# One decoder layer on one core: two weight splits behind a sigmoid, one low part behind three sums, five convolution taps ahead of the row copies

## The chip, the cores and the metric

The kernel runs on one core of a Trainium2 chip. The metric is the device time of one execution in microseconds (us), the median over several runs. Engines are named as the profile names them: PE (TensorE, matmuls), DVE (VectorE), ACT (ScalarE), POOL (GpSimd) and SP (SyncE, which issues the loads).

## The reference

One layer of a decoder for 512 prompt tokens and 64 sample tokens (8 sequences of 8), all in one pass, 576 tokens in all. Everything is in 32-bit floats.

```python
x = x + 0.5 * swiglu_ffn(x, norm_ffn1, ffn1_w_gu, ffn1_w_down)
h = rmsnorm(x, norm_mix)
glu_in, q_a, c_kv, k_pe, gate_a, gate_b = split(h @ w_in)
u = ga * sigmoid(gb)                    # the two halves of glu_in
y_conv = conv_branch(u, ...)            # causal depthwise conv (31 taps), layernorm, silu, projection
y_attn = latent_attention(q_a, c_kv, k_pe, cached pages) @ w_attn_out
m = sigmoid(gate_a) * y_conv + sigmoid(gate_b) * y_attn
x = x + m @ w_out
x = x + 0.5 * swiglu_ffn(x, norm_ffn2, ffn2_w_gu, ffn2_w_down)
```

D_MODEL is 1024, D_FF 2816, the convolution has 512 channels, the latent part of `w_in` 672 columns and each gate 1024.

## The kernel before

Activations stand transposed, channels on the 128 partitions and the 576 tokens along the row, in two halves of 288. A product of 32-bit values is made from three faster ones: each operand is split into a high part and a low part (the rest), and PE adds high x high, high x low and low x high.

**Chunks.** The weights come in tiles of 128 columns, called chunks: SP loads one into one of four raw buffers (`load_chunk`), ACT copies it into one of two high buffers (`split_hi`, L442 to 447), POOL subtracts that from the raw tile in four pieces, which gives the low part (`split_lo`, L454), and PE makes 48 matmuls of it (`chunk`, `product`, L468). `split_hi` of chunk n waits until PE has used chunk n-2, since there are two high buffers. PE's next chunk waits for the low part and for one of four pairs of PSUM banks, which is free when DVE has read the result of four units before (`unit_read`).

**The mixing stage.** The chunks of `w_in` follow each other without a pause: eight for the GLU (`n_glu`, pairs j = 0 to 3), six for the latent rows (`n_lat`), sixteen for the gates (`n_gate`). For each GLU pair DVE scales both results out of PSUM (`scaled`, L1861), ACT applies the sigmoid (`glu`, L1024) and DVE multiplies. After that come `sample_conv` (for the sample tokens: one product of 1984 elements per partition, L2087, and a sum, L2089) and taps of the prompt convolution (`taps`, L2071 and L2074), which DVE has to do at some time and which are dealt out between the other steps. The numbers `AT_LAT`, `AT_GATE` and `AT_GATE2` say which tap comes where: five behind each of the gates 0 to 6, five in another place (below), four behind each of the last four gates. For a gate DVE scales the result, ACT applies the sigmoid (`gate`, L1039).

Behind gate 7 PE transposes the latent rows back in five groups of six (L1477, 128 tokens each, the last 64), each into its own pair of banks; DVE copies each out (L2160, L2161). The fifth group needs the pair that the first row copy frees, gate 8's chunk the one of the second. Then POOL fills `lat_ss`, ACT squares and sums the rows (L1065, L1066), DVE makes the norms, and the gates 8 to 11 run beside it.

**The feed-forward stages.** The first three pairs of columns run as plain chunks. The other nineteen, called units, are made from seven products of half size instead of eight (L1390, twelve matmuls each, in the order GATE1, GATE2, SUM_G, SUM_U, DIF, REST, UP2). For each unit SP loads the gate columns (`w_raw`, L573) and the up columns (`up_rows`, L578); DVE makes four sums of them (`weight_sums`, `last_weight_sum`, L1817 to L1827); ACT makes the high parts (`weight_hi`, L896); DVE makes the low parts of GATE1, GATE2, SUM_G (`weight_low`, L1911) and of UP2 (`up2_low`, L1917), POOL the others (L730). `combine` adds the seven results. All of DVE's work on unit u+1 is dealt out between the `combine`s of unit u; for unit 0 this order is written out in `first_seven`. There is one `up_rows` buffer: SP's load of it for unit u+1 waits for `up2_low` of unit u, and in SP's queue the gate columns of unit u+2 stand behind that load.

```python
if not first or u or f:
    sp.wait_ge(up2_lo, unit_sums(f, u, 1, 0))
for half, k0 in enumerate((0, KH)):
    dst = up_rows[:, half, :].rearrange("p (k c) -> p k c", c=P)
    sp.dma_start(dst, wv[:, k0:k0 + KH, ds(of(u, P, PLAIN[f] * P + DFF), P)]).then_inc(up_in, 16)
```

**The cached pages.** Behind the attention of the prompt SP issues 16 loads of `c_nat` and 16 of `kpe_nat` for the first sequence. The first wait for `prep_q`, which DVE signals with `rope_rep`.

Of the kernel before, what the change touches and what calls it, by code (L numbers as in the profile page):

```python
# [22 lines left out]
P = 128  # L23
D = 1024
KD = D // P
# [21 lines left out]
LATC = -(-LAT // P)  # L47
# [13 lines left out]
RAWS, HIS = 4, 2  # L61
# [32 lines left out]
def layer(nc, x_prompt, x_sample, cache_ckv, cache_kpe, state_conv, page_table, w, const, out):  # L94

    ctx = ExitStack()
    with ctx:
# [255 lines left out]
        GLU_TAPS, LAT_TAPS, GATE_TAPS, GATE2_TAPS = 4, 5, 5, 4  # L353
        AT_LAT = (CT - 1) * GLU_TAPS
        AT_GATE = AT_LAT + (LATC - 1) * LAT_TAPS
        AT_GATE2 = AT_GATE + KD * GATE_TAPS
# [9 lines left out]
        n_lat = n_glu + 2 * CT  # L366
# [29 lines left out]
        def of(u, m, c):  # L396

            return m * u + c if isinstance(u, int) else u[0] * (2 * m) + (m * u[1] + c)
# [6 lines left out]
        def unit_sums(f, u, m, c):  # L405

            return of(u, m, m * U0[f] + c)
# [9 lines left out]
        def seven_bank(f, slot):  # L417

            return (4 + IN_ORDER.index(slot)) % 8
# [18 lines left out]
        def arrived(n, r):  # L438

            return 32 * (n // RAWS + 1) if isinstance(n, int) else (n - r) * (32 // RAWS) + 32  # L440

        def split_hi(act, n, r, size, free=True):  # L442

            act.wait_ge(w_in_sem[r], arrived(n, r))
            if free:
                act.wait_ge(w_used, n - (HIS - 1))
            act.activation(w_hibuf[:, r % HIS, 0:size], w_rawbuf[:, r, 0:size], ACT.Copy).then_inc(w_hi_done, 1)  # L447
# [391 lines left out]
        def _(act):  # L839
# [182 lines left out]
            def glu(j):  # L1022
                act.wait_ge(unit_read, glu_base(j) + 2 * j + 2)
                act.activation(tb[:, :], tb[:, :], ACT.Sigmoid).then_inc(sigmoid_done, 1)  # L1024

            for j in range(CT - 1):
                if j:
                    up_hi(n_glu, j + 1, j + 1)
                glu(j)
            for n in (n_lat, n_lat + 1):  # L1030
                split_hi(act, n, n % RAWS, KD * P)
            glu(CT - 1)
            for c in range(2, LATC):
                n = n_lat + c
                split_hi(act, n, n % RAWS, KD * min(P, LAT - c * P))

            def gate(g, q0=q_gate):
                act.wait_ge(unit_read, g + (q0 + 1))
                act.activation(gates[:, ds(g, 1), :], gates[:, ds(g, 1), :], ACT.Sigmoid).then_inc(sigmoid_done, 1)  # L1039

            def gate_hi(g, gmod):
                split_hi(act, g + n_gate, (n_gate + gmod) % RAWS, KD * P)

            gate_hi(0, 0)
            gate_hi(1, 1)
            with act.Fori(0, KD // 4) as i:
                for c in range(4):
                    gate_hi(i * 4 + (c + 2), c + 2)
                    gate(i * 4 + c)

            steps = [0]

# [9 lines left out]
            for i in range(NT):  # L1062
                n = P if i < PT_TILES else TS
# [12 lines left out]
            for i in range(NT):  # L1076
                n = P if i < PT_TILES else TS
# [707 lines left out]
        def _(dve):  # L1785
# [65 lines left out]
            for g in range(NX):  # L1851
                n = X_GROUPS[g][1]
# [60 lines left out]
            def up2_low(f, u, b):  # L1913

                dve.wait_ge(w7_sum, unit_sums(f, u, 4, 1))
                dve.wait_ge(w7_hi, unit_sums(f, u, 7, HI_ORDER.index(UP2) + 1))
                dve.tensor_tensor(w7[b][:, UP2, 1, :], up_rows[:, 1, :], w7[b][:, UP2, 0, :].bitcast(F32), ALU.subtract).then_inc(up2_lo, 1)  # L1917

            def combine(f, u, slot):

                n = IN_ORDER.index(slot) + 1
                dve.wait_ge(w7_used, unit_sums(f, u, 7, n))
                got = ps[:, seven_bank(f, slot), 0:HALF]
                lo, hi = slice(0, HALF), slice(HALF, T)
                if slot == GATE2:
                    dve.wait_ge(part_read, unit_sums(f, u, 1, 1))
                    dve.wait_ge(a_made, of(u, 1, FT * f + PLAIN[f]))
                    dve.tensor_tensor(ta[:, lo], got, parts[:, 1, :], ALU.add).then_inc(c_done, 1)
                elif slot == SUM_G:
                    dve.tensor_tensor(parts[:, 2, :], got, parts[:, 1, :], ALU.add).then_inc(c_done, 1)  # L1930
                elif slot == SUM_U:
                    dve.wait_ge(c_done, unit_sums(f, u, 7, 2))
                    dve.tensor_tensor(parts[:, 0, :], got, parts[:, 2, :], ALU.add).then_inc(c_done, 1)
                elif slot == DIF:
                    dve.wait_ge(c_done, unit_sums(f, u, 7, 3))
                    dve.tensor_tensor(tb[:, hi], got, parts[:, 0, :], ALU.add).then_inc(c_done, 1)
                    dve.tensor_tensor(parts[:, 2, :], got, parts[:, 2, :], ALU.add).then_inc(c_done, 1)
                elif slot == REST:
                    dve.tensor_tensor(ta[:, hi], got, parts[:, 0, :], ALU.add).then_inc(c_done, 1)
                else:  # L1940
                    dve.wait_ge(c_done, unit_sums(f, u, 7, 5))
                    dve.tensor_tensor(tb[:, lo], got, parts[:, 2, :], ALU.add).then_inc(c_done, 1)
# [25 lines left out]
            def first_seven(f):  # L1968

                weight_sums(f, 1, 1)  # L1970
                weight_low(f, 1, 1, GATE1)
                up2_low(f, 1, 1)
                combine(f, 0, GATE2)
                last_weight_sum(f, 1, 1)
                weight_low(f, 1, 1, GATE2)
                combine(f, 0, SUM_G)
                weight_low(f, 1, 1, SUM_G)
                combine(f, 0, SUM_U)
                combine(f, 0, DIF)
                combine(f, 0, REST)  # L1980

# [111 lines left out]
            def taps(n0, n1):  # L2093

                for n in range(n0, n1):
                    if n % W == 0:
                        dve.wait_ge(ext_done, n // W + 1)
                    tap(n // W, n % W, n if n % W else None)
# [37 lines left out]
            def gate(g, q):  # L2136

                dve.wait_ge(w_used, n_gate + g + 1)
                scaled(gates[:, g, :], q % 4).then_inc(unit_read, 1)
                if g < KD - 1:  # L2140
                    taps(AT_GATE + GATE_TAPS * g, AT_GATE + GATE_TAPS * (g + 1))
                elif g >= KD + 4:
                    taps(AT_GATE2 + GATE2_TAPS * (g - KD - 4), AT_GATE2 + GATE2_TAPS * (g - KD - 3))

            for c in range(8):
                gate(c, q_gate + c)
# [9 lines left out]
            for i in range(NT):  # L2156
                n = P if i < PT_TILES else TS
# [1 line left out]
                dve.wait_ge(tr_done, KD + 4 + i)  # L2159
                dve.tensor_copy(lat[0:n, i, 0:512], ps[0:n, 2 * s, :])  # L2160
                dve.tensor_copy(lat[0:n, i, 512:LAT], ps[0:n, 2 * s + 1, 0:LAT - 512]).then_inc(unit_read, 1)  # L2161
            taps(AT_GATE + GATE_TAPS * (KD - 1), AT_GATE2)
            gate(KD, q_gate2)
            dve.wait_ge(filled, 3)
            dve.wait_ge(ss_done, NT)
# [20 lines left out]
            for i in range(NT):  # L2186
                n = P if i < PT_TILES else TS
                dve.tensor_scalar(lat[0:n, i, 0:QL], lat[0:n, i, 0:QL], lat_ss[0:n, 0, i:i + 1], None, ALU.mult)
                c = lat[0:n, i, QL:QL + KL]
# [5 lines left out]
            for i in range(NT):  # L2195
                n = P if i < PT_TILES else TS
# [9 lines left out]
            for i in range(NT):  # L2206
                n = P if i < PT_TILES else TS
# [392 lines left out]
```

## Time and profile before

| | |
|---|---|
| median of 3 runs | 1602.19 us (1600.95 to 1603.7) |
| the profiled execution | 1603.7 us, of it span in the trace 1601.9 us |
| PE busy | 1572.9 us, 98% of the span |
| DVE, ACT, POOL busy | 1043.6, 628.3, 575.4 us (65%, 39%, 36%) |
| mean granted clock of PE | 0.995 |
| loaded from HBM | 117.79 MB, 76 GB/s over the span with what is written |

The span is that of one execution, taken by the hardware profiler; the time of the run is a little longer. Busy shares are means over all stages. Times in the text such as "at 480.32" are microseconds from the start of the span. Ends of matmuls are modelled, so two rows that follow each other may overlap by 0.15 us.

### The profile page before, as it was taken

How to read it: one execution, taken by the hardware profiler on the slowest of the kernel's cores; microseconds unless marked ns; L12 is line 12 of the kernel's file. 1: busy time of each engine (PE TensorE's matmuls, PEld its weight loads, DVE VectorE, ACT ScalarE, POOL GpSimd, SP SyncE). 2: the span in 40 equal slices, each digit the busy share in tenths (PEclk: the TensorE clock that was granted, in tenths of full speed). 3: DMA queues.
4: the chain of work that ended last, by engine and by line, in shares of the span. 5: the costliest groups of instructions: out<-in, count | busy, mean ns of one | idle time of the engine just before them, and what ended most of it. 6: DMA issues, size and time to landing. Idle time of an engine off the chain costs nothing.

```text
span 1601.9 us, 32058 instructions
## 1 busy us (share of the span) xinstructions
PE 1572.9 (98%) x11330; PEld 1495.8 (93%) x11330; DVE 1043.6 (65%) x1674; ACT 628.3 (39%) x1168; POOL 575.4 (36%) x604
## 2 busy tenths in 40 slices
PE   9999999999999999998999999999999999999997
PEld 8999999999999998687988888888999999999997
DVE  4998888521279966664877777774549988884001
ACT  5443435322221241363544445552335444353110
POOL 2065555454446644220000000002561654554441
PEclk9999999999999999998999999999999999999999
DMA  5133334232233421002122222211231332342321
GB/s 158 51 99 99 91 92 125 63 91 73 78 85 104 122 70 56 1 2 66 53 61 60 59 59 53 53 42 53 84 111 56 93 105 83 100 115 65 89 73 59
DMA packets 230106, 122.24 MB, mean 76 GB/s; under 512 B 28255, under 2 KB 227015, under 8 KB 230004
## 3 DMA queue, kind: packets, MB, share of 16 engines
q1 hardware_dynamic: 229182, 120.56, 26.8%
q8 instruction: 52, 0.85, 0.2%
q10 hardware_dynamic: 830, 0.48, 0.1%
q14 instruction: 42, 0.34, 0.1%
HBM read 117.79 MB, written 3.58 MB: 76 GB/s over the span
## 4 chain that ended last, share of the span: by engine, by line
PE 85%; DVE 8%; issue 3%; ACT 2%; SPq 1%; DVEq 0%; DMA 0%; POOL 0%; ACTq 0%; POOLq 0%
PE ps L468 38%; PE ps L1390 25%; PE ps L1703 8%; PE ps L1641 4%; PE ps L1275 1%; PE ps L1501 1%; DVE xs L1905 1%; PE ps L1627 1%; PE ps L1526 1%; PE ps L1508 1%; DVE page_ss L2498 1%; PE ps L1551 1%; SPq L657 1%; SPq L660 1%; ACT sq L1196 1%
## 5 line engine op out<-in xcount | busy, mean ns | idle before, releaser
L454 POOL TENSOR_TENSOR w_lobuf<-w_rawbuf,w_hibuf 128x256 fp32r<-128x256 f32 (+2 forms) x336 | 313.8, 965 | 360.1 <-ACT w_hibuf L447 360.1
L1390 PE MATMUL ps<-xs,w 128*128 128x288 f32 x3192 | 429.4, 296 | 5.7 <-DVE w L1911 4.5
L1390 PEld LDWEIGHTS ps<-xs,w 128*128 128x128 f32 x3192 | 427.0, 188 | 7.8 <-issue 7.8
L730 POOL TENSOR_TENSOR w<-w_raw,w 128x256 fp32r<-128x256 f32 x216 | 219.7, 1049 | 233.9 <-DVE w_raw L1821 153.1
L447 ACT ACTIVATE w_hibuf<-w_rawbuf 128x1024 fp32r<-128x1024 f32 (+1 forms) x90 | 104.8, 1164 | 357.4 <-PE ps L468 356.6
L2045 DVE SCALAR_TENSOR_TENSOR xT<-ps,xT 128x576 f32<-128x576 f32 x24 | 18.2, 758 | 228.5 <-PE ps L468 228.5
L468 PE MATMUL ps<-a_hi,w_lobuf 128*128 128x288 f32 x704 | 152.2, 297 | 0.0
L468 PE MATMUL ps<-a_hi,w_hibuf 128*128 128x288 f32 x704 | 152.1, 296 | 0.0
L468 PE MATMUL ps<-a_lo,w_hibuf 128*128 128x288 f32 x704 | 150.3, 294 | 0.0
L468 PE MATMUL ps<-x_hi,w_hibuf 128*128 128x288 f32 (+1 forms) x672 | 145.7, 298 | 1.1 <-DVE cT L2202 0.7
L468 PE MATMUL ps<-x_lo,w_hibuf 128*128 128x288 f32 (+1 forms) x672 | 144.2, 296 | 0.0
L468 PE MATMUL ps<-x_hi,w_lobuf 128*128 128x288 f32 (+1 forms) x672 | 144.1, 296 | 0.0
L896 ACT ACTIVATE w<-w_raw 128x512 fp32r<-128x512 f32 x228 | 128.2, 622 | 10.9 <-DVE w_raw L1817 5.8
L1703 PE MATMUL ps<-kq_hi,cT_hi 128*128 128x288 f32 x512 | 117.3, 310 | 1.0 <-ACT sq L1196 0.9
L2498 DVE TENSOR_REDUCE page_ss<-sq 128x8 f32<-128x512 f32 x128 | 83.5, 675 | 49.6 <-ACT sq L1196 49.5
L468 PEld LDWEIGHTS ps<-a_hi,w_hibuf 128*128 128x128 f32 x704 | 113.7, 189 | 0.0
L468 PEld LDWEIGHTS ps<-a_lo,w_hibuf 128*128 128x128 f32 x704 | 113.0, 188 | 0.0
L468 PEld LDWEIGHTS ps<-a_hi,w_lobuf 128*128 128x128 f32 x704 | 112.7, 188 | 0.0
L1911 DVE TENSOR_TENSOR w<-w_raw,w 128x512 fp32r<-128x512 f32 x120 | 110.1, 917 | 0.1
L1703 PE MATMUL ps<-kq_hi,cT_lo 128*128 128x288 f32 x512 | 110.0, 296 | 0.0
L1703 PE MATMUL ps<-kq_lo,cT_hi 128*128 128x288 f32 x512 | 109.9, 296 | 0.0
L468 PEld LDWEIGHTS ps<-x_hi,w_hibuf 128*128 128x128 f32 (+1 forms) x672 | 107.1, 186 | 2.2 <-issue 1.4
(312 smaller groups left out, 2683.8 us busy)
## 6 DMA issues: line engine op xcount, KB each, us to landing
w_raw<-in_ffn_w_gu SPq DMA_DIRECT2D x76, 256.0 KB, 2.9
up_rows<-in_ffn_w_gu SPq DMA_DIRECT2D x76, 256.0 KB, 3.1
c_nat<-in_cache_ckv SPq DMA_DIRECT2D x128, 128.0 KB, 2.0
w_rawbuf<-in_w_in SPq DMA_DIRECT2D x58, 256.0 KB, 3.2
w_rawbuf<-in_ffn_w_down SPq DMA_DIRECT2D x32, 384.0 KB, 4.1
w_rawbuf<-in_ffn_w_down SPq DMA_DIRECT2D x32, 320.0 KB, 3.4
w_rawbuf<-in_ffn_w_gu SPq DMA_DIRECT2D x24, 256.0 KB, 3.4
w_rawbuf<-in_w_out SPq DMA_DIRECT2D x16, 256.0 KB, 3.0
```

The lines of the kernel that those rows point to most:

```text
L447: act.activation(w_hibuf[:, r % HIS, 0:size], w_rawbuf[:, r, 0:size], ACT.Copy).then_inc(w_hi_done, 1)
L454: ins = pool.tensor_tensor(w_lobuf[:, r, part], w_rawbuf[:, r, part], w_hibuf[:, r % HIS, part].bitcast(F32), ALU.subtract)
L468: mm = pe.matmul(ps[0:width, 2 * s + h, 0:HALF], a, b[:, k, h * HALF:(h + 1) * HALF], start=first and i == 0 and j == 0, stop=last and i = ...
L657: return sp.value_load(pages[0:1, ds(s * NP + t, 1)], min_val=0, max_val=cache_ckv.shape[1] - 1)
L730: ins = pool.tensor_tensor(w7[b][:, slot, 1, part], w7_raw[b][:, slot, 1, part], w7[b][:, slot, 0, part].bitcast(F32), ALU.subtract)
L896: act.activation(w7[b][:, slot, 0, :], src, ACT.Copy).then_inc(w7_hi, 1)
L1390: mm = pe.matmul(ps[:, seven_bank(f, slot), 0:HALF], m, xs[:, slot, n, k, :], start=k == 0 and j == 0, stop=k == KH - 1 and j == 2)
L1641: mm = pe.matmul(ps[0:HQ, 7, 0:KL], s_buf[:, b, t, :], c_nat[:, b, t, :], start=t == 0, stop=False)
L1703: mm = pe.matmul(ps[:, page_banks(t) + half, 0:KQ], a, m[:, half, cols], start=k == 0 and j == 0, stop=k == 1 and j == 2)
L1911: dve.tensor_tensor(w7[b][:, slot, 1, :], w7_raw[b][:, slot, 1, :], w7[b][:, slot, 0, :].bitcast(F32), ALU.subtract).then_inc(w7_lo, 1)
L2045: dve.scalar_tensor_tensor(x2, unit(s), scale, x2, op0=ALU.mult, op1=ALU.add).then_inc(x_done, 1)
L2498: dve.tensor_reduce(page_ss[:, t, :], sq[:, u, 0:H * DN].rearrange("p (h d) -> p h d", d=DN), AX, ALU.add).then_inc(page_red, 1)
```

## The change

Four pieces of work change their place; none is added or removed. On ACT the split of latent chunk 1 goes behind the sigmoid of the last GLU pair, and in the loop over the first eight gates the split of chunk k+2 goes behind the sigmoid of gate k. On DVE `up2_low` for unit 1 goes behind `combine(f, 0, SUM_U)` in both feed-forward stages, and the five taps that stood behind the five row copies go behind gate 7, ahead of them.

```diff
@@ ScalarE @@
-            for n in (n_lat, n_lat + 1):
-                split_hi(act, n, n % RAWS, KD * P)
+            split_hi(act, n_lat, n_lat % RAWS, KD * P)
             glu(CT - 1)
-            for c in range(2, LATC):
+            for c in range(1, LATC):
                 n = n_lat + c
                 split_hi(act, n, n % RAWS, KD * min(P, LAT - c * P))
...
             gate_hi(0, 0)
-            gate_hi(1, 1)
             with act.Fori(0, KD // 4) as i:
                 for c in range(4):
-                    gate_hi(i * 4 + (c + 2), c + 2)
+                    gate_hi(i * 4 + (c + 1), c + 1)
                     gate(i * 4 + c)
+            gate_hi(KD + 1, KD + 1)
@@ VectorE @@
                 weight_sums(f, 1, 1)
                 weight_low(f, 1, 1, GATE1)
-                up2_low(f, 1, 1)
                 combine(f, 0, GATE2)
                 last_weight_sum(f, 1, 1)
                 weight_low(f, 1, 1, GATE2)
                 combine(f, 0, SUM_G)
                 weight_low(f, 1, 1, SUM_G)
                 combine(f, 0, SUM_U)
+                up2_low(f, 1, 1)
                 combine(f, 0, DIF)
                 combine(f, 0, REST)
...
-                if g < KD - 1:
+                if g < KD:
                     taps(AT_GATE + GATE_TAPS * g, AT_GATE + GATE_TAPS * (g + 1))
...
-            taps(AT_GATE + GATE_TAPS * (KD - 1), AT_GATE2)
             gate(KD, q_gate2)
```

## Rows read from the trace of the kernel before

**Rows 1.** Busy time of PE, from the page

```profile
PE 1572.9 (98%) x11330; PEld 1495.8 (93%) x11330; DVE 1043.6 (65%) x1674; ACT 628.3 (39%) x1168; POOL 575.4 (36%) x604
```

**Rows 2.** Stretch 409 to 600: busy PE, PEld, DVE, ACT, POOL, clock, DMA share, GB/s

```profile
409.00:600.00 191.00, 191.00 (x1437) 188.69 (x1437) 142.02 (x178) 51.37 (x74) 101.52 (x115) 1.00 0.34 93
```

**Rows 3.** Timeline, start of feed-forward 1: start, length, engine, line, operation

```profile
80.07 1.22 DVE L1917 TENSOR_TENSOR w<-up_rows,w 128x512 fp32r<-128x512 f32 x1
...
87.91 0.69 DVE L1817 TENSOR_TENSOR w_raw<-up_rows 128x512 f32<-128x512 f32 x1
...
91.97 0.85 DVE L1911 TENSOR_TENSOR w<-w_raw,w 128x512 fp32r<-128x512 f32 x1
...
80.29 1.85 PE L1390 MATMUL ps<-xs,w 128*128 128x288 f32 x12 [0.70 <-DVE w L1911]
83.70 200.80 PE L1390 MATMUL ps<-xs,w 128*128 128x288 f32 x1500 [1.56 <-DVE w L1911]
...
81.46 0.93 SPq L578 DMA_DIRECT2D up_rows<-in_ffn_w_gu  x2
```

**Rows 4.** Landing of two `w_raw` loads at 66.87, the first of a train

```profile
DMA to landing us min/median/max: 2.8/3.2/3.6
```

**Rows 5.** Timeline and chain, latent chunks (the last row: chain)

```profile
480.32 0.69 ACT L1024 ACTIVATE tb<-tb 128x576 f32<-128x576 f32 x1 [0.79 <-DVE tb L1861]
483.03 2.21 DVE L2087 TENSOR_TENSOR s_prod<-ext,cols 128x1984 f32<-128x1984 f32 x1
492.41 4.82 POOL L454 TENSOR_TENSOR w_lobuf<-w_rawbuf,w_hibuf 128x256 fp32r<-128x256 f32 x4 [3.59 <-ACT w_hibuf L447]
...
452.77 63.97 PE ps L468 x480
```

**Rows 6.** Timeline, gates 6 and 8: sigmoid, split, low part, taps

```profile
563.12 5.33 DVE L2074 SCALAR_TENSOR_TENSOR y<-ext,cols,y 128x512 f32<-128x512 f32 x5
573.84 3.88 DVE L2074 SCALAR_TENSOR_TENSOR y<-ext,cols,y 128x512 f32<-128x512 f32 x5
579.57 0.76 DVE L1861 TENSOR_TENSOR gates<-ps,rstd 128x576 f32<-128x576 f32 x1 [1.85 <-PE ps L468]
...
562.45 1.06 ACT L447 ACTIVATE w_hibuf<-w_rawbuf 128x1024 fp32r<-128x1024 f32 x1 [4.77 <-PE ps L468]
580.37 0.69 ACT L1039 ACTIVATE gates<-gates 128x576 f32<-128x576 f32 x1 [0.90 <-DVE gates L1861]
580.96 1.04 ACT L447 ACTIVATE w_hibuf<-w_rawbuf 128x1024 fp32r<-128x1024 f32 x1
...
563.59 4.32 POOL L454 TENSOR_TENSOR w_lobuf<-w_rawbuf,w_hibuf 128x256 fp32r<-128x256 f32 x4 [2.22 <-ACT w_hibuf L447]
582.08 2.82 POOL L454 TENSOR_TENSOR w_lobuf<-w_rawbuf,w_hibuf 128x256 fp32r<-128x256 f32 x4 [7.91 <-ACT w_hibuf L447]
```

**Rows 7.** Timeline, gate 7 and the row transposes

```profile
568.84 0.76 DVE L1861 TENSOR_TENSOR gates<-ps,rstd 128x576 f32<-128x576 f32 x1 [0.39 <-PE ps L468]
569.56 0.69 DVE L2160 COPY lat<-ps 128x512 f32<-128x512 f32 x1
570.17 0.31 DVE L2161 COPY lat<-ps 128x160 f32<-128x160 f32 x1
...
568.64 4.30 PE L1477 MATMUL ps<-ident,latT 128*128 128x128 f32 x30
```

**Rows 8.** PE at the first cached pages: one stretch, then the timeline

```profile
743.97:750.79 6.82, 3.44 (x15) 3.44 (x16) 1.35 (x2) 0.60 (x1) 0.00 (x0) 0.50 0.11 17
...
742.89 0.33 PE L1664 MATMUL ps<-ident,kpe_nat 128*128 128x128 f32 x1 [1.22 <-DMA kpe_nat<-in_cache_kpe]
747.35 1.11 PE L1627 MATMUL ps<-ident,c_nat 128*128 128x128 f32 x4 [4.13 <-DMA kpe_nat<-in_cache_kpe]
748.74 0.68 PE L1703 MATMUL ps<-kq_lo,cT_hi 128*128 128x288 f32 x2
749.22 0.68 PE L1703 MATMUL ps<-kq_hi,cT_lo 128*128 128x288 f32 x2
```

## The prediction

> **What bounds the kernel now.** I read the profile in the order page, chain, stretches, timeline. The page says PE is busy 1572.9 of 1601.9 us [rows 1], so only what makes PE wait can cost much, and only 29 us of PE's idleness can ever be won. Then the stretches: between 409 and 600 us, where three of the four edits lie, PE is busy 191.00 of 191.00 us at clock 1.00 [rows 2]. Nothing is to be won there; the question for each edit is how much slack stands between a helper engine and PE's need. The fourth edit lies at the start of both feed-forward stages, where PE does wait: 0.70 and 1.56 us, each time for VectorE's low weight parts [rows 3].
>
> **`up2_low` in `first_seven` (VectorE, twice).** Now it runs at 80.07 for 1.22 us, before the op that the 1.56 us wait ends with [rows 3]. It moves behind `combine(SUM_U)`. GATE2's low part then comes about 1.15 us earlier (the 1.22 less the little by which two ops overlap), and the second product of unit 1 starts at 82.55, not 83.70 [rows 3]: 1.15 us won. But SyncE's load of the next `up_rows` waits for `up2_low`: it issues at 81.46 now [rows 3]. In the new order three combines (0.4 each), the last weight sum (0.9) and two low parts (1.0 and 0.8) stand before it, counted from 80.07, and it takes itself the 0.85 of a low part [rows 3]: it ends at 84.7 (an estimate from the lengths of these ops now), and the issue comes at 84.9. The second of the two loads is issued 0.46 us after the first (half of 0.93 [rows 3]). In the new order both gate loads of unit 3 are free by then and follow at once; at the head of such a train two loads took 2.8 and 3.6 us to land, 3.2 in the middle [rows 4]. Landing: 85.35 + 3.2 to 3.6 = 88.6 to 89.0, about 88.9 with its semaphore. VectorE wants `up_rows` at 87.91 [rows 3], so it is 1.0 us late. From there to the end of unit 2's first low part is 91.97 + 0.85 - 87.91 = 4.91 us [rows 3]: 93.8, and PE can start at 93.95. Before, unit 2 starts at 83.70 plus six products: 1500 matmuls took 200.80 us, 0.134 each, 1.6 us for the twelve of a product [rows 3], so 93.3. The 1.15 us won turn into a wait of 1.8 us one unit later, net +0.65 us. Later units wait for nothing now (all 1500 matmuls stand in one row [rows 3]), so VectorE has room to catch up. Feed-forward 2 runs the same code and begins with the same two waits. Both stages: +1.3 us; bounds -2.3 (landing never late) and +2.4 (landing 0.5 us later still).
>
> **Latent tile 1 split behind the last GLU sigmoid (ScalarE).** The sigmoid waits for VectorE and starts at 480.32 [rows 5]; the split, now at 478.47, would start 0.59 us after it (the step from sigmoid to split in [rows 6]), at 480.91, and GpSimd 1.14 us later (split 562.45, GpSimd 563.59 [rows 6]), at 482.05. Queued behind it there is VectorE's product of the sample convolution, 2.21 us, starting at 483.03 at the latest, perhaps at 482.1 [rows 5]. When GpSimd met that same product at 492.41 its four pieces took 4.82 us instead of 2.82 [rows 5, 6]. So the low part is done at 482.05 + 4.85 = 486.9 to 487.1 and PE can start at 487.15. PE wants it five chunks after 452.77, at 6.40 us a chunk (63.97 us for ten) [rows 5]: 484.75. Cost +2.4 us; bounds +0.6 (four pieces at 0.7) and +3.5.
>
> **Gates: split after sigmoid instead of before.** Per gate the sigmoid follows VectorE's read by 0.80 us, the split the sigmoid by 0.59, GpSimd the split by 1.14 [rows 6]: GpSimd starts 2.5 us after the read, where it now starts 1.14 after. Now its pieces run beside VectorE's taps and take 4.32 us [rows 6], to 567.91; PE wants the tile at 568.64 [rows 7]: slack 0.6 after 0.14 us of signalling. In the new order two taps are over before GpSimd starts, so I take two and a half pieces at 1.15 (five taps beside GpSimd 5.33 us, alone 3.88 [rows 6]) and the rest at 0.7: done 6.6 us after the read, PE 6.72 after. The read comes 0.2 us after the next chunk's start, so PE wants it 6.2 after: 0.5 us late. A late chunk gives the chunk behind it that time back, since its own split hangs on an earlier read; so only gates 2, 4 and 6 stall, and gate 8 has the row transposes ahead. 3 x 0.53 = +1.6 us; bounds 0 and +4.1. The Trainium skill (SBUF — State Buffer, "Who interferes with whom") says that such a pair of VectorE and GpSimd instructions takes an exclusive lock for the whole instruction. Strictly alternating, a tap of 0.75 and a piece of 0.7 would take 1.45 us per pair, but the trace shows 1.15, so they overlap in part. By the page the stall would be 1.35 us and this term 4.1; I keep 1.6 and carry the page's as a rival.
>
> **Five taps ahead of the row copies (VectorE).** Now the copies start 0.72 us after the read of gate 7 [rows 7]. In the new order five taps come first: 5.28 us after the read they are over (three alone at 0.78, two beside GpSimd at 1.15, from 0.67). Queued behind them are all five row copies, and for the first waits PE's fifth group of transposes, for the second the chunk of gate 8. A copy pair takes 0.92 us (two copies in [rows 7]), so row 0 is read 6.17 after, at 575.0; PE needs it at 572.06 (four of the five groups of the 4.30 us row, 0.87 each, from 568.64 [rows 7]). With the second row's copy the chunk of gate 8 starts at 576.0 instead of 572.87: +3.2 us; bounds +3.0 and +3.9 (all taps beside GpSimd). The taps cost nothing where they were: VectorE waited 1.85 us behind them [rows 6]. ScalarE's squares of the rows also start 4.5 us later and end at 584.1, so gate 10's split starts at 584.6 and its low part ends at 588.6, 0.2 before PE wants it: hidden, but barely.
>
> **The clock.** PE would stand still for 3.1 us at the row copies and for 2.4 us at latent tile 1. After waits of 1.22 and 4.13 us the granted clock was 0.50 for 6.8 us [rows 8], the lower of its two levels, 1.2 GHz; a pair of matmuls then starts every 0.48 us [rows 8]. The waits of 0.70 and 1.56 us that stand close together [rows 3] did not lower it. The new stalls lie between these. At full clock a pair takes 6.40/24 = 0.267 us [rows 5]. A low stretch half as long as that one costs 3.4 x (1 - 0.267/0.48) = 1.5 us. I take one such fall, +1.5; bounds 0 and +3. The Trainium skill (TensorE: Matmul & The Clock Gate, "What's actually happening") says that the lower level is the default and that recent activity releases it; the trace agrees.
>
> **Sum.** 1.3 + 2.4 + 1.6 + 3.2 + 1.5 = +10.0 us. The profiled execution took 1603.7 us (span 1601.9 and 1.8 around it), 1.5 over the median of the runs, 1602.2. Forecast for a median: 1612.2 us.
>
> **The rivals.**
> - *All stalls, no fall of the clock:* 1610.7. For it: the stalls are shorter than 4.13 us. 0.25.
> - *The clock falls two or three times:* 1613.7 to 1615.2. Two long stalls and two of 1.8 us give it occasion. 0.12.
> - *GpSimd keeps up:* the ScalarE swaps (2.4 and 1.6) are hidden, 1608.2. Against it: the slack in the gates is 0.6 us and the move 1.4. 0.10.
> - *Full lock:* each gate stall is 1.35 us, 1614.7. Against it the 1.15 us pairs. 0.05.
> - *The load of `up_rows` is not late:* the two gains of 1.15 stay, 1.3 turns into -2.3, 1608.6. Against it the 2.8 us of even the quickest landing [rows 4]. 0.03.
> - *Not slower:* at the first cached pages PE waits 1.22 + 4.13 us for a load of keys [rows 8]. Did that load not start behind PE, PE's lateness would vanish there: with the clock held, 8.5 - 5.35 = 3.15 us remain, 1605.3, within 0.2%. This decides once more than 5.3 us are given back. Against it: in the code SyncE's string of page loads waits for VectorE's `rope_rep`, which stands behind the attention heads, so the wait moves along. 0.05.
>
> **How the numbers follow.** The forecast has 0.40 (its own range 1610 to 1614), the rivals 0.60 together. 0.2%, 3.2 us, is about what a measurement of this kernel can tell from no change. Slower holds all but the last rival: 0.94; same 0.05; faster 0.01, which no case makes. From the first stall alone to all bounds, 1606.5 to 1616.
>
> **What would show it.** PE's waits in the changed profile: one of 2.4 us near 485 for GpSimd's `w_lobuf`; three of about 0.5 us every second gate; one of 3.1 us inside the row transposes for `lat`; in each feed-forward stage 0.4 instead of 1.56 us, then 1.8 us a unit later, with `up_rows` issued at 84.9. PE's clock below 1.00 behind the row copies. I am wrong if GpSimd's pieces run faster beside VectorE than the rows show, or if a stall is absorbed by a wait that is already there.

## The result, and the profile after

The changed kernel takes 1618.56 us (median of 4 runs, 1617.94 to 1620.24); the kernel before took 1602.94 on the same chip. The ratio is 1.0098, with a 95% interval of 1.0083 to 1.0113. The forecast of slower holds; the time lies 2.6 us above 1616, the top of the range: +15.6 us where +10.0 was forecast. The profiled run took 1619.69 us, 16.0 more than the profiled run of before.

First the totals. These are the busy times of the changed kernel's page, which answer to [rows 1], and below them its list of what PE waited for (us in total, times, the longest). Line numbers of the changed kernel are mostly one lower than before.

```profile
PE 1583.2 (98%) x11330; PEld 1504.7 (93%) x11330; DVE 1037.1 (64%) x1674; ACT 628.3 (39%) x1168; POOL 572.4 (35%) x604
```

```profile
PE ps L1389 <- DVE w L1910: 7.5, 6, 3.2
PE ps L1626 <- DMA kpe_nat<-in_cache_kpe: 3.8, 1, 3.8
PE ps L468 <- POOL w_lobuf L454: 3.1, 4, 2.1
PE ps L1476 <- DVE lat L2160: 2.8, 1, 2.8
```

PE is busy 10.3 us longer with the same 11330 matmuls. The waits are not in that number. A good part of it is matmuls at the lower clock, so this row already hints that the clock took more than the forecast gave it.

Then the start of feed-forward 1, the timeline, which answers to [rows 3].

```profile
84.13 0.85 DVE L1916 TENSOR_TENSOR w<-up_rows,w 128x512 fp32r<-128x512 f32 x1
...
90.90 0.69 DVE L1816 TENSOR_TENSOR w_raw<-up_rows 128x512 f32<-128x512 f32 x1 [3.18 <-DMA up_rows<-in_ffn_w_gu]
...
80.56 1.85 PE L1389 MATMUL ps<-xs,w 128*128 128x288 f32 x12 [0.70 <-DVE w L1910]
82.83 9.93 PE L1389 MATMUL ps<-xs,w 128*128 128x288 f32 x72 [0.43 <-DVE w L1910]
95.93 4.44 PE L1389 MATMUL ps<-xs,w 128*128 128x288 f32 x22 [3.16 <-DVE w L1910]
...
85.15 0.93 SPq L578 DMA_DIRECT2D up_rows<-in_ffn_w_gu  x2
86.33 0.99 SPq L573 DMA_DIRECT2D w_raw<-in_ffn_w_gu  x2
```

The wait of 1.56 us is down to 0.43, as the prediction had it, and `up_rows` is issued at 85.15. But VectorE gets it at 90.90 only, and PE stands still for 3.16 us. How long the two loads took to land (the view of the tile `up_rows`, 85.1 to 86.0), and what the queues carried from 85.71 to 88.3 (packets, MB, share of the sixteen engines):

```profile
DMA to landing us min/median/max: 3.3/4.2/5.2
```

```profile
q1 hardware_dynamic: 1073, 0.54, 71.6%
q8 instruction: 1, 0.02, 2.2%
```

The second load took 5.2 us. One 16 KB instruction load (a piece of an engine's program, fetched from memory) lay in its window. In feed-forward 2 there was none until the load had landed; its second load took 3.6 us and PE waited 2.03.

The mixing stage: latent chunk 1 (answers to [rows 5]), gate chunks 2, 4 and 6, and gate 7 with the row transposes ([rows 6, 7]).

```profile
484.33 0.69 ACT L1024 ACTIVATE tb<-tb 128x576 f32<-128x576 f32 x1 [7.19 <-DVE tb L1860]
484.92 1.04 ACT L447 ACTIVATE w_hibuf<-w_rawbuf 128x1024 fp32r<-128x1024 f32 x1
...
537.09 0.40 PE L468 MATMUL ps<-x_hi,w_hibuf 128*128 128x288 f32 x1 [0.34 <-POOL w_lobuf L454]
550.49 0.53 PE L468 MATMUL ps<-x_hi,w_hibuf 128*128 128x288 f32 x2 [0.34 <-POOL w_lobuf L454]
563.89 0.52 PE L468 MATMUL ps<-x_hi,w_hibuf 128*128 128x288 f32 x2 [0.35 <-POOL w_lobuf L454]
...
576.97 0.76 DVE L1860 TENSOR_TENSOR gates<-ps,rstd 128x576 f32<-128x576 f32 x1 [1.11 <-PE ps L468]
577.65 4.58 DVE L2073 SCALAR_TENSOR_TENSOR y<-ext,cols,y 128x512 f32<-128x512 f32 x5
582.14 0.68 DVE L2159 COPY lat<-ps 128x512 f32<-128x512 f32 x1
...
579.57 3.92 POOL L454 TENSOR_TENSOR w_lobuf<-w_rawbuf,w_hibuf 128x256 fp32r<-128x256 f32 x4 [2.42 <-ACT w_hibuf L447]
...
583.11 1.46 PE L1476 MATMUL ps<-ident,latT 128*64 128x128 f32 x6 [2.85 <-DVE lat L2160]
```

Each wait stands where the prediction put it: the split of chunk 1 starts 0.59 us behind the sigmoid and PE waits 2.07 for its low part, three gates are late by a third of a microsecond, and the row copies start 5.17 us after the read of gate 7, behind five taps.

Last the clock: PE busy, PEld, DVE, ACT, POOL, granted clock, DMA share and GB/s in five stretches.

```profile
42.81:46.22 3.41, 3.41 (x15) 3.41 (x16) 3.37 (x6) 1.60 (x3) 0.00 (x0) 0.50 0.00 0
97.40:100.80 3.40, 3.40 (x16) 3.40 (x16) 2.89 (x6) 1.56 (x3) 2.04 (x3) 0.50 0.46 129
486.00:492.00 6.00, 3.93 (x29) 3.70 (x29) 5.93 (x5) 1.06 (x1) 5.96 (x6) 1.00 0.31 87
...
582.10:588.90 6.80, 5.79 (x24) 5.24 (x25) 4.27 (x11) 2.27 (x9) 1.60 (x4) 0.50 0.00 1
...
1271.60:1275.00 3.40, 3.40 (x17) 3.40 (x16) 3.13 (x6) 0.60 (x2) 2.99 (x4) 0.50 0.46 135
```

Behind three of the new waits the granted clock is 0.50 (1.2 GHz), for 3.4, 6.8 and 3.4 us; behind the wait of 2.07 us at 490.85 it stays at 1.00. The first row is a fall that comes ahead of all four edits: PE runs the same instructions there as in the kernel before, where the clock is 1.00, and has no wait over 0.3 us.

**The bill.** It is read by following the same instructions through both traces: how much later each of them starts than before.

| place | forecast | measured: waits | measured: clock |
|---|---|---|---|
| feed-forward 1, start | 0.65 | 2.4 | 1.4 |
| latent chunk 1 | 2.4 | 2.3 | 0 |
| gates 2, 4, 6 | 1.6 | 1.8 | 0 |
| row copies and gate 8 | 3.2 | 3.0 | 2.4 |
| feed-forward 2, start | 0.65 | 1.1 | 1.5 |
| one fall of the clock | 1.5 | | |
| sum | 10.0 | 10.6 | 5.3 |

A wait of 0.34 us costs a gate 0.6, since the ends of matmuls are modelled and a wait shows shorter than the next start is late; the column holds what the starts show. At the row copies the clock is already at 0.50 when the last six transposes run: the chunk of gate 8 starts 3.5 us later than before, of it 3.0 for the wait (what is left in run 4, where the clock stays up) and the rest for the clock. Together 15.9; 0.3 more come from the start of the layer and 0.2 less from attention, where nothing was edited. These small rests hide more of the clock: the fall at 42.8 cost 1.5 us, and at the cached pages the clock is at 0.50 for 13.7 us where it was for 10.2 before. Two terms are off: the feed-forward waits, 3.5 where 1.3 stood, and the clock, 5.3 where 1.5 stood. The clock column is that of one execution.

### The profile page after: what moved, and what is told of

Its sections match the earlier page's. It is cut to its first block, busy times and chain, and to the rows that moved or that the text cites. A ratio compares the mean times of both kernels' runs of the same rounds, so it can differ in the third digit from the quotient of the medians.

```text
span 1617.9 us, 32058 instructions
## 1 busy us (share of the span) xinstructions
PE 1583.2 (98%) x11330; PEld 1504.7 (93%) x11330; DVE 1037.1 (64%) x1674; ACT 628.3 (39%) x1168; POOL 572.4 (35%) x604
## 4 chain that ended last, share of the span: by engine, by line
PE 79%; DVE 9%; issue 5%; ACT 2%; POOL 2%; SPq 1%; DMA 1%; DVEq 0%; ACTq 0%; POOLq 0%
PE ps L468 33%; PE ps L1389 24%; PE ps L1702 9%; PE ps L1640 3%; POOL w_lobuf L454 2%; PE ps L1274 1%; PE ps L1500 1%; PE ps L1626 1%; DVE xs L1904 1%; PE ps L1525 1%; PE ps L1507 1%; PE ps L1550 1%; SPq L657 1%; DVE y L2073 1%; DVE page_ss L2496 1%
## 5 line engine op out<-in xcount | busy, mean ns | idle before, releaser
L1389 PEld LDWEIGHTS ps<-xs,w 128*128 128x128 f32 x3192 | 430.0, 189 | 10.6 <-DVE w L1910 5.7
```

What stands on the lines that cost most here:

```text
L1389: mm = pe.matmul(ps[:, seven_bank(f, slot), 0:HALF], m, xs[:, slot, n, k, :], start=k == 0 and j == 0, stop=k == KH - 1 and j == 2)
```

## The experiments

Each run is compared with the kernel before on its own chip. Intervals are at 95%.

**1. `up2_low` alone.** The first question is whether this edit alone makes its share, or only together with the others.

```diff
                 weight_low(f, 1, 1, GATE1)
-                up2_low(f, 1, 1)
                 combine(f, 0, GATE2)
...
                 combine(f, 0, SUM_U)
+                up2_low(f, 1, 1)
```

> Only the move of up2_low behind combine(SUM_U) in first_seven; the other three edits are not made. Theory A (the feed-forward term was mis-sized because the second up_rows load lands late, and the clock falls after the wait that follows): PE waits 0.43 us for GATE2 of unit 1 and then 2.0 to 3.2 us for GATE1 of unit 2 in each stage, and the clock is 0.50 for about 3.4 us behind at least one of them; 3.5 to 6.3 us over the kernel before, 1606.5 to 1609. Rival B (the term was right, +1.3 us, and what is over belongs to an interplay with the edits of the mixing stage): 1604.2.

Measured: 1607.21 us, ratio 1.0025 (1.0013 to 1.0036). The timeline of PE in feed-forward 1:

```profile
80.33 1.86 PE L1390 MATMUL ps<-xs,w 128*128 128x288 f32 x12 [0.69 <-DVE w L1911]
82.61 9.94 PE L1390 MATMUL ps<-xs,w 128*128 128x288 f32 x72 [0.42 <-DVE w L1911]
95.43 4.85 PE L1390 MATMUL ps<-xs,w 128*128 128x288 f32 x23 [2.89 <-DVE w L1911]
```

The long wait is there without the other edits, with the clock at 0.50 from 95.5 to 98.9. The second load landed in 4.9 us, again with an instruction load 2.2 us behind its issue.

**2. The other three edits, without `up2_low`.**

```diff
-            for n in (n_lat, n_lat + 1):
-                split_hi(act, n, n % RAWS, KD * P)
+            split_hi(act, n_lat, n_lat % RAWS, KD * P)
...
-                    gate_hi(i * 4 + (c + 2), c + 2)
+                    gate_hi(i * 4 + (c + 1), c + 1)
...
-                if g < KD - 1:
+                if g < KD:
                     taps(AT_GATE + GATE_TAPS * g, AT_GATE + GATE_TAPS * (g + 1))
```

> The three edits of the mixing stage without the move of up2_low. Theory A: stalls of 2.1, 3 x 0.34 (0.6 with the restart) and 2.9 us as in the changed kernel, and a fall of the clock behind the last: 9.6 us over the kernel before, 1612.5, so that this and e_up2 add up to the changed kernel. Rival B (interplay): the sum of the two differs from 15.6 by more than 2 us. Rival C (the clock's fall is not tied to the stall): 7.6 us over.

Measured: 1612.82 us, ratio 1.0064 (1.0047 to 1.0081). The waits of the mixing stage are those of the changed kernel, within 0.01 us: 2.08, 0.34, 0.35, 0.34 and 2.85. The two halves, 4.95 and 10.56 us over their kernel before, make 15.5 of 15.6. The intervals of the two are about 3.7 and 5.5 us wide, so the times alone would leave room for some interplay between the stages; the waits, equal within 0.01 us, show none.

**3. Gate loads held back.** The prediction had asked only about the gate loads behind `up_rows` as what could lengthen its landing. Here SyncE issues those of unit 3 only when `up_rows` of unit 2 has landed.

```diff
-                with sp.Fori(0, (SEVEN[f] - 3) // 2) as i:
+                load_seven(f, wv, 2, 0)
+                sp.wait_ge(up_in, 32 * (U0[f] + 3))
+                load_seven(f, wv, 3, 1)
+                with sp.Fori(1, (SEVEN[f] - 3) // 2) as i:
```

> As e_up2, and SyncE issues the gate loads of unit 3 only when the up_rows of unit 2 have landed. Theory A1 (up_rows land late because the two gate loads issued behind them share the DMA queues): the second up_rows load lands 3.0 to 3.3 us after its issue instead of 3.6 to 5.2, PE waits about 1.7 us at unit 2, the clock stays at 1.00, and the whole is about 1 us over the kernel before, 1604. Rival A2 (they land late only because they are issued 3.5 us later, whatever runs beside them): landing and time as in e_up2.

Measured: 1605.04 us, ratio 1.0017 (1.0007 to 1.0026). In feed-forward 2 the second load landed in 3.4 us instead of 3.5 and PE's wait fell to 1.24. In feed-forward 1 it still took 4.7 us, PE waited 2.55, and against the expectation the clock fell, for 6.8 us. So the gate loads are not what makes the landing long there. What remained in the window was the instruction load. It ran from 86.24 to 87.23. The queues from 84.2 to 87.2, and behind the dots from 87.2 to 88.5:

```profile
q1 hardware_dynamic: 1023, 0.51, 58.0%
q8 instruction: 1, 0.02, 2.1%
...
q1 hardware_dynamic: 33, 0.02, 7.2%
```

The second load is 1056 packets. By the time the instruction load ended, 1023 of them were done or under way; the other 33 followed one behind the other until 88.44, at a rate of about one busy engine of the sixteen (7.2%).

**4. PE kept busy at the row copies.** The changed kernel with twelve matmuls of ones (24 rows of the trace) ahead of the fourth group of row transposes. They compute nothing that is used.

```diff
                 pe.wait_ge(unit_read, q - 3)
+                if i == NT - 2:
+                    keep_busy(12, ps[:, 2 * s, 0:P])
```

> The changed kernel with 12 matmuls of ones (2.8 us) on PE ahead of the fourth group of row transposes, into banks that the group then overwrites, so that PE is busy while VectorE does the five taps. Theory A (the fall of the clock for 6.8 us behind the row copies comes from PE standing still there): no wait over 0.4 us at the row transposes, granted clock 1.00 behind them, gate 8's chunk 6.4 us long again, 2.0 us under the changed kernel: 1616.5. Rival C (the fall has another cause): the fall stays and the time is that of the changed kernel.

Measured: 1616.66 us, ratio 1.0091 (1.0075 to 1.0108). That is 14.4 us over the kernel before on its chip, where the changed kernel had 15.6; the intervals overlap, so the time alone shows no gain, and the trace has to. From 575 to 590 PE is busy 14.82 of 15.00 us at clock 1.00, and from the gates before 560 to those after 600 the lateness grows by 3.7 us instead of 6.1. The lower clock there was a price of its own, on top of the late copies. The clock fell elsewhere: for 6.8 us in feed-forward 1, behind a wait of 3.08. In feed-forward 2 it did not fall, behind a wait of 2.65.

**5 and 6. The two kernels of 1 and 3 with 51 warming matmuls instead of 36.** The matmuls of ones stand at the start of the program, and more of them shift the instruction loads against the work.

```diff
-WARM = 36
+WARM = 51
```

> e_up2 with 51 instead of 36 warming matmuls at the start of PE's program. The 15 more come before the first product, so the kernel starts about 2 us later, and PE's later instructions, and the 16 KB loads of them that the trace shows about every 17 us, lie elsewhere against up_rows. Theory F (in feed-forward 1 the last part of up_rows is late because such a load of 16 KB, at 87.6 in e_up2, holds up one DMA engine while up_rows come in): with that load at about 84 the second up_rows load lands at most 3.8 us after its issue instead of 4.9, and PE waits at most 1.9 us at unit 2 of feed-forward 1 instead of 2.9. Theory A1 (the two gate loads behind it make it late): landing 4.9 and wait 2.9 stay. The run's total is about 2 us over e_up2 in either case for the longer start, less what is won.

> e_up2_alone (gate loads of unit 3 held back until up_rows have landed) with 51 warming matmuls. Theory F: with neither gate loads nor an instruction load beside it the second up_rows load of feed-forward 1 lands in 3.0 to 3.3 us, PE waits 1.2 to 1.7 us at unit 2, and the clock stays at 1.00 there. Theory A1 with F wrong: landing as in e_up2_alone, 4.7 us.

Measured, in two executions of each: 1610.78 and 1610.84 us, both 1.0055 (1.0035 to 1.0075). The instruction load did not leave the window as expected; it moved to 0.6 and 0.2 us before the issue of the second load, which landed in 4.2 and 4.1 us. PE waited 2.25 and 1.81; behind the 1.81 the clock fell for 3.4 us, against the expectation. In feed-forward 2 it moved into the window, 1.9 and 2.3 us behind the issue: the landings there grew from 3.5 and 3.4 to 4.5 and 4.9 us, the waits from 1.84 and 1.24 to 2.85 and 2.64, and the clock fell, for 6.8 and 3.4 us. What was meant to shorten one landing lengthened the other. Beside this the kernel starts 2 to 3 us later.

**7. The taps alone.** The last edit of the diff by itself.

> Only the five taps ahead of the row copies. Theory A (VectorE's taps hold up the copy that frees the banks of the fifth group; beside GpSimd's subtractions a tap takes 1.15 us): one wait of PE of 3.4 to 3.8 us at the row transposes, longer than the 2.85 us of the changed kernel since GpSimd now runs beside more of the taps, then a fall of the clock that costs up to 2.0 us: 4.0 to 6.0 us over the kernel before. Rival G (taps take the same time with GpSimd beside them or not): the wait is 2.85 us as in the changed kernel.

Measured: 1608.52 us, ratio 1.0037 (1.0025 to 1.005), 6.8 us over the kernel before, above the 6.0 expected. The wait is 3.55 us, as theory A had it, and not the 2.85 of rival G. VectorE, GpSimd and PE at gate 7:

```profile
569.86 5.28 DVE L2074 SCALAR_TENSOR_TENSOR y<-ext,cols,y 128x512 f32<-128x512 f32 x5
...
570.38 4.21 POOL L454 TENSOR_TENSOR w_lobuf<-w_rawbuf,w_hibuf 128x256 fp32r<-128x256 f32 x4 [2.13 <-ACT w_hibuf L447]
...
576.02 1.46 PE L1477 MATMUL ps<-ident,latT 128*64 128x128 f32 x6 [3.55 <-DVE lat L2161]
```

GpSimd runs beside nearly all five taps here, and they take 5.28 us. In the changed kernel it starts 1.9 us behind the first tap, because the gate's split stands behind the sigmoid, and the taps take 4.58. So the two edits do act on each other inside this stage: the ScalarE edit takes 0.7 us off the price of this one.

**8. The cached pages.** All kernels wait at the first pages [rows 8], and the rival "not slower" hung on that wait. Here eight pages of `c_nat` are loaded, then eight of `kpe_nat`, then the rest in turns, instead of all `c_nat` first.

```diff
-            for t in range(NP):
+            for t in range(8):
                 load_page(cache_ckv, c_nat, ckv_in, page_of(0, t), 0, t)
...
             sp.wait_ge(uk_split, 1)
-            for t in range(NP):
+            for t in range(8):
+                load_page(cache_kpe, kpe_nat, kpe_in, page_of(0, t), 0, t)
+            for t in range(8, NP):
+                load_page(cache_ckv, c_nat, ckv_in, page_of(0, t), 0, t)
                 load_page(cache_kpe, kpe_nat, kpe_in, page_of(0, t), 0, t)
```

> The kernel before with the page loads of the first sequence in another order: 8 of c_nat, then 8 of kpe_nat as soon as their place is free, then the other 8 of each in turn. Theory H (PE's waits of 1.22 and 4.13 us at the first pages are set by SyncE's string of loads, 1.09 us each, which starts behind the attention heads; so PE's lateness moves along and is not given back there): the kpe_nat loads start at about 732.4 instead of 737.6, both waits nearly go, at most 1 us remains, and the clock does not fall behind them; 4 to 6 us under the kernel before, 1597. Rival I (the waits are set by something else, the landing or PE's own preparation): no gain.

Measured: 1596.2 us (5 runs, 1595.45 to 1596.83), ratio 0.9962 (0.9948 to 0.9977). Both waits are gone: the first `kpe_nat` is issued at 732.14 where it was 737.64. Below, the timeline of PE, and behind the dots a stretch as in [rows 8].

```profile
734.18 1.11 PE L1630 MATMUL ps<-ident,c_nat 128*128 128x128 f32 x4
735.09 3.62 PE L1278 MATMUL ps<-ones 128*128 128x128 f32 x16
738.50 0.72 PE L1630 MATMUL ps<-ident,c_nat 128*128 128x128 f32 x4
...
731.92:738.75 6.83, 6.83 (x34) 6.71 (x34) 4.04 (x9) 1.50 (x3) 0.00 (x0) 0.50 0.10 15
```

The expectation that the clock would stay up was wrong: it is at 0.50 for 6.8 us (10.2 in the kernel before), and PE is busy throughout. This is the lowest ratio of the study. In the changed kernel, with the old order, the first `kpe_nat` is issued at 751.07, 13.4 us later than before; the wait at the pages was still 3.84 us, and of 13.6 us of lateness 0.2 were given back.

**9 and 10. `up2_low` at an earlier place, and both improvements together.** If only the late issue of `up_rows` spoils the edit, `up2_low` could stand directly behind the low part of GATE2, so that PE's first wait shrinks and the load is still early.

```diff
                 weight_low(f, 1, 1, GATE1)
-                up2_low(f, 1, 1)
                 combine(f, 0, GATE2)
                 last_weight_sum(f, 1, 1)
                 weight_low(f, 1, 1, GATE2)
+                up2_low(f, 1, 1)
                 combine(f, 0, SUM_G)
```

The same is done in the loop over the later units, where it goes behind the low part of GATE1.

> The kernel before with up2_low of the next unit directly behind the low part of GATE2 in both first_seven orders (before: ahead of it; changed kernel: behind combine of SUM_U). If the wait before unit 1's second product hangs on up2_low standing ahead of GATE2's low part, that wait falls from 1.56 to about 0.43 us as in the changed kernel. If what then goes wrong in the changed kernel is only that the load of up_rows comes too late, here it is issued at 83 to 83.5 us (two and a half combines earlier than 84.9), lands even after 4.2 us by 87.7, ahead of VectorE's need at 87.9, and no wait of 2 to 3 us follows at unit 2 and the clock stays up: 1.1 us less per stage, 1599.5 to 1601.5. Rival: the load lands later than 4.5 us beside the gate loads and the instruction load, VectorE waits 0.5 to 1 us, and the time is that of the kernel before within 0.1%.

> The page loads reordered as in the run before (first eight of c_nat, eight of kpe_nat, then alternating), and up2_low directly behind the low part of GATE2 in both first_seven orders. If the two places are independent, the savings add: 1593.5 to 1595.5 (6 us for the pages, 1 to 2.3 for the feed-forward starts). Rival: the gain of the feed-forward starts is nothing or given back: 1596 to 1597.

Measured: 1603.29 us, ratio 1.0002 (0.9993 to 1.0011), and 1597.13 us, ratio 0.9968 (0.9956 to 0.998). PE in feed-forward 1 of the first:

```profile
79.08 1.87 PE L1390 MATMUL ps<-xs,w 128*128 128x288 f32 x12 [0.69 <-DVE w L1911]
81.36 1.87 PE L1390 MATMUL ps<-xs,w 128*128 128x288 f32 x12 [0.41 <-DVE w L1911]
83.64 199.75 PE L1390 MATMUL ps<-xs,w 128*128 128x288 f32 x1488 [0.41 <-DVE w L1911]
```

The first load is issued at 82.53, the second lands at 86.39, before VectorE wants it (86.72), and no long wait follows. Still nothing is won: 0.41 us come back before the next product, and from the start of the second product (81.36, before 83.70) to the end of the stage the same 1500 matmuls take 1.2 us longer than in [rows 3], in pauses too short for rows of their own. The rival had the time right and the cause wrong: it had the load land late. What takes the gain back is not shown. VectorE works without a pause from 86.72 to beyond 93, so its sums and low parts may set PE's pace there in whatever order they stand; the changed order in the loop was not tried apart from the one in `first_seven` either. In run 10 nothing was added to the gain of the pages: it lies 5.6 us under its kernel before, run 8 5.5 us under its own.

**11 and 12. The kernels of 1 and 3 with 24 warming matmuls.** By then the landings could be sorted (the table below), and fewer warming matmuls should move the instruction load behind the window.

```diff
-WARM = 36
+WARM = 24
```

> up2_low behind combine of SUM_U alone, with 24 warming matmuls ahead of the layer where there were 36 (51 in the run before). Over the nine profiles so far the second load of up_rows landed in 2.9 to 3.7 us (median 3.2) 277 times with nothing beside it, in 3.3 to 4.2 (median 3.6) with gate loads right behind, and in 4.1 to 5.2 (median 4.8, 12 times) where a 16 KB instruction load started up to 2.5 us behind its issue. That load started 2.0 to 2.2 us behind the issue with 36 warming matmuls and 0.6 before it with 51, so with 24 it should start 3.5 to 4.5 us behind it in feed-forward 1. If it is the instruction load that makes the landing long: the second load of up_rows lands in 3.3 to 3.7 us there, PE's second wait is 1.2 to 1.8 us instead of 2.89, and its clock stays at 1.00 (or falls only briefly). Rival: the landing is long because of what is queued at this point of the stage, whatever the instruction loads do: 4.9 us and a wait of 2.9 us.

> The same with the gate loads held back until up_rows has landed, and 24 warming matmuls. If instruction load and gate loads are the two causes: landing 3.0 to 3.4 us in feed-forward 1 and PE's second wait 0.9 to 1.4 us (2.55 with 36 warming matmuls, landing 4.7). Rival: 4.7 again.

Measured: 1604.03 us, ratio 1.0012 (1.0 to 1.0023), and 1601.83 us, ratio 0.9998 (0.9987 to 1.0009). In feed-forward 1 the second load landed in 3.2 us in both. PE in the first of them:

```profile
78.50 1.85 PE L1390 MATMUL ps<-xs,w 128*128 128x288 f32 x12 [0.70 <-DVE w L1911]
80.78 9.85 PE L1390 MATMUL ps<-xs,w 128*128 128x288 f32 x72 [0.43 <-DVE w L1911]
91.96 108.26 PE L1390 MATMUL ps<-xs,w 128*128 128x288 f32 x808 [1.34 <-DVE w L1911]
```

A wait of 1.34 instead of 2.89, no fall of the clock, and the stage costs 0.4 us instead of 3.5. What was changed is a constant at the start of the program, none of the loads. In the second the wait is 1.04 and the stage costs 0.1. In feed-forward 2 of the first PE waited 2.19 for a load that landed in 3.8 us, and the clock held. These comparisons rest on the traces: the shorter start alone puts both kernels 1.8 us ahead of the kernel before, so the ratios look better than the edit is.

**The landings of eleven profiles.** For every unit in the kernels before and after, 1, 3 to 6 and 9 to 12, the second load of `up_rows`, sorted by what lay beside it:

| beside the load | loads | landing, us |
|---|---|---|
| nothing | 343 | 2.8 to 3.7, median 3.2 |
| two gate loads right behind | 9 | 3.2 to 4.2, median 3.6 |
| an instruction load, from 0.3 us before to 2.5 behind the issue, no gate loads | 7 | 4.1 to 5.0, median 4.7 |
| both | 5 | 4.3 to 5.2, median 4.9 |

The first two units of each stage, whose load has other loads ahead of it in the queue, are left out: these 44 took 3.8 to 5.8 us, all but two without an instruction load beside them. Ten with one gate load behind took 3.0 to 4.0. The bounds of the third row were drawn after the landings were seen, and the 4.2 in the second row is feed-forward 1 of run 5, where an instruction load began 0.6 us before the issue; the other eight took 3.2 to 3.9. The three profiles that the table leaves out (2, 7 and 8) have one load each beside an instruction load: 4.6, 4.0 and 4.9 us.

## Why the prediction was wrong, point by point

**What bounds the kernel:** right. In the full stretch nothing was won, and what the edits cost there is how much later a helper's result came than PE wanted it, and the clock.

**`up2_low`: the first half right, the landing wrong.** The 1.15 us won (82.83 where 82.55 plus 0.27 of late start was forecast) and the issue (85.15 against 84.9) came as worked out. The step that failed is "85.35 + 3.2 to 3.6 = 88.6 to 89.0": the second load landed at 90.9. It took 5.2 us (4.9 in run 1), outside even the bound of 0.5 us more. The range 3.2 to 3.6 was drawn from data loads ([rows 4]) and asked only which other data loads stood beside it. The gate loads cost 0.4 us by the table; the instruction load costs 1.5. Runs 11 and 12 show that: the instruction load moves out of the window, the data loads around stay in their order, and the landing falls to 3.2 us. The rest of the working then held: from VectorE's start at 90.90 to PE at 95.93 are 5.03 us, where 4.91 and 0.15 were taken. In feed-forward 2, without an instruction load, the landing was 3.6 and the net cost 1.1 us, half a microsecond over the 0.65. Most of it is the step "0.46 us after the first": in this stage the two loads are issued 0.88 us apart (1261.51 and 1262.39), in the kernel before too (1244.66 and 1245.54). The prediction took feed-forward 1 for both.

**Latent chunk 1:** right, 2.3 us for 2.4. Four pieces beside the sample convolution took 4.77 us; 4.85 was taken.

**Gates:** right in place and number, 1.8 us for 1.6, the number with some luck. The traces show each wait as 0.34 us, and the chunk behind it 0.6 later. GpSimd is done 6.6 us after the read (557.19 to 563.76), as forecast; but 2.5, two and a half pieces at 1.15 and the rest at 0.7 add up to 6.4, which would have given 1.0 us and not 1.6. The rival of a full lock, 1.35 us per gate, is excluded, since a gate stalls by less than half of that. The Trainium skill (SBUF — State Buffer, "Who interferes with whom") calls contention between VectorE and GpSimd an exclusive lock and counts such a pair under it; that the lock lasts the whole instruction it says of VectorE's 2-port modes. For this pair the trace does not agree with a lock of that length.

**Five taps ahead of the row copies:** right, 3.0 us for 3.2 with the clock's share taken out. Alone the edit gives a wait of 3.55 (run 7), in company 2.85: the ScalarE edit moves GpSimd behind the first taps. The sum had this in it, with three taps alone and two beside GpSimd, 4.6 us; they took 4.58.

**The clock: "I take one such fall" failed.** Behind the new waits there were three, and they cost 5.3 us, above the bound of 3: one lasted 6.8 us, twice the length taken. The rival that had them ("two or three times", 0.12) was the right one in kind; with its 1613.7 to 1615.2 it took 1.5 us for each, which fits two of the three (the long one cost 2.4), and it stood on feed-forward waits that were too short. Waits forecast at 1.8 us were 3.16 and 2.03. In all profiles of the study the waits of 2.85 us and more that the edits made were each followed by a clock of 0.50, those of 1.34 and less by none; between them 1.81, 2.03, 2.55 and 2.64 were, and 1.84, 2.07, 2.19, 2.25 and 2.65 were not. Length alone does not decide it. Nor is a wait needed: the clock fell at 42.8 in the changed kernel, at 43.3 in run 2 and 43.1 in run 7, and not in the other profiles, in a piece of the program that none of them changes. And executions of one kernel differ: those of run 1 have mean clocks of 0.991 to 0.995 and take 1602.85 to 1608.22 us, those of the changed kernel 0.989 to 0.991. So the count of falls in one profile is partly chance. What decides a fall was not tried and stays open.

**The range:** its top does not follow from the terms. The upper bounds 2.4, 3.5, 4.1, 3.9 and 3 add up to 16.9 us, which makes 1619.1 and not 1616. The measured time lies inside that sum, though two of its terms, the feed-forward waits and the clock, went beyond their own bounds.

**"Not slower":** rightly given little. The wait at the pages moved along with PE (3.84 us left), since the loads wait for `rope_rep` (13.4 us later, for 13.6 of lateness).

How the causes are held apart: that the instruction load lengthens the landing is shown (runs 5, 6, 11, 12, in both directions). That it does so by holding up one of the sixteen DMA engines fits the packets of run 3, of which the last 33 follow in single file right behind it; the trace does not name the engine of a packet, so this last step is argued.

## What to carry to other kernels

When an edit shortens the slack of a load, take its landing time from the worst neighbour that the trace shows, instruction loads included, and ask what follows if the resulting wait also costs the clock: here the two together made 6.4 us of a term of 1.3. A gap that seems to come from one operation standing in the wrong place may only be where a busy helper's lateness shows; run 9 took the wait named by the trace from 1.56 to 0.41 us and won nothing. And look at what is untouched: the largest gain, 5.5 us, lay in the order of the page loads, far from the change.

## What the runs showed of the hardware

- The program comes in instruction loads of 16 KB, one every 18 to 20 us in the first 107 us of the changed kernel (queue q8: 52 loads in the run). They move when the number of PE's matmuls is changed (runs 5, 6, 11, 12), so they are PE's. The Trainium skill (Runtime: NRT & Kernel Launch, "Instruction fetch mechanics") names blocks of this size, fetched through a DMA queue of the sequencer's own, and a cost that is mostly hidden. The trace agrees on the block and on PE: no wait of PE over 0.3 us in the changed kernel is without another releaser. The kernel before has one of 0.68 us, at 73.9 beside a load that began at 73.5, but run 5 has the like at 76.2 with no instruction load within 10 us. For a data load beside it, the cost was 1.5 us.
- Changing 36 to 24 or 51 matmuls in the first 12 us shifted these loads by 2 us or more against the work at 85 us, and moved the cost of that stage, with its clock, between +0.4 and +3.5 us (+1.3 with 51; one profile each). A difference of 0.2% between two kernels can be this alone.
- A piece of GpSimd and a tap of VectorE side by side took 4.2 us for four and 5.28 for five; with GpSimd starting two taps later 3.92 and 4.58.
